# A decoder step with a 32-expert mixture: expert weights in 2 MiB pieces of 16 KB rows, and the scatter to tokens in fp32r parts

## The reference

```python
    def expert_block(args):
        xblk, e = args
        gu = xblk.astype(F32) @ w_gate_up[e].astype(F32) + b_gate_up[e].astype(F32)
        gate, up = gu[:, :D_FF], gu[:, D_FF:]
        gate = jnp.minimum(gate, SWIGLU_LIMIT)
        up = jnp.clip(up, -SWIGLU_LIMIT, SWIGLU_LIMIT)
        glu = gate * jax.nn.sigmoid(SWIGLU_ALPHA * gate)
        return ((up + 1.0) * glu) @ w_down[e].astype(F32) + b_down[e].astype(F32)

    yb = lax.map(expert_block, (xb, block_expert)).reshape(n_rows, -1)
    y = jax.ops.segment_sum(yb * gate_of_row[:, None], token_of_row, num_segments=T + 1)[:T]
```

## Time and profile before

| | us |
|---|---|
| median of 3 runs | 1326.84 |
| the 3 runs | 1319.71, 1326.84, 1328.22 |
| the profiled execution's own time | 1317.78 |
| its span, first to last instruction | 1316.1 |
| PE busy | 1264.1 (96%) |
| DMA, 400 to 1200 us | 421 GB/s at a busy share of 1.01 |

### The profile page before, as it was taken

The page is one execution under the profiler, slowest core; times in us unless marked ns, Lnnn a source line. Parts: engine busy times, 40 slices in busy tenths (PEclk is TensorE's granted clock), DMA queues, the critical chain, the costliest instruction groups (busy, mean ns, idle before and its releaser), DMA issues.

```text
span 1316.1 us, 18528 instructions
## 1 busy us (share of the span) xinstructions
PE 1264.1 (96%) x7834; PEld 570.1 (43%) x7834; DVE 396.4 (30%) x828; ACT 236.5 (18%) x500; POOL 30.9 (2%) x81
## 2 busy tenths in 40 slices
PE   7999999999999999999999999999999999998896
PEld 5777878854533333333333333333333333332232
DVE  2266756645411222122122213112221212121123
ACT  2114243411312011111111111111111111111112
POOL 6000000000010000000000000000000000000000
PEclk9999699999999999999999999999999999999999
DMA  9732111272599999999999999999999999999995
GB/s 266 165 97 65 33 42 67 67 271 74 195 399 422 421 421 420 420 422 420 420 421 421 420 420 421 420 421 423 420 420 420 421 421 421 421 420 420 422 410 188
DMA packets 77212, 436.91 MB, mean 332 GB/s; under 512 B 11892, under 2 KB 27319, under 8 KB 32072
## 3 DMA queue, kind: packets, MB, share of 16 engines
q1 hardware_dynamic: 75048, 431.11, 81.3%
q0 software_dynamic: 1040, 3.54, 0.9%
q10 hardware_dynamic: 1040, 1.05, 0.3%
HBM read 430.79 MB, written 4.89 MB: 331 GB/s over the span
## 4 chain that ended last, share of the span: by engine, by line
PE 72%; DMA 26%; DVE 1%; issue 1%; SPq 0%; ACT 0%; ACTq 0%; DVEq 0%
PE bank L1330 22%; DMA ring<-in_w_gate_up 17%; PE bank L1353 11%; PE bank L731 11%; DMA ring<-in_w_down 8%; PE bank L1312 6%; PE bank L1383 5%; PE bank L1136 3%; PE bank L1344 2%; PE bank L911 1%; PE bank L1372 1%; PE bank L859 1%; PE bank L758 1%; PE bank L888 0%; PE bank L955 0%
## 5 line engine op out<-in xcount | busy, mean ns | idle before, releaser
L1330 PE MATMUL bank<-ring,mix 128*64 128x512 f32 x2048 | 473.2, 598 | 16.4 <-DMA ring<-in_w_gate_up 16.0
L1330 PEld LDWEIGHTS bank<-ring,mix 128*64 128x64 f32 x2048 | 136.9, 136 | 320.7 <-issue 275.8
L1353 PE MATMUL bank<-ring,mix 128*64 128x512 f32 x1024 | 234.0, 598 | 8.0 <-DMA ring<-in_w_down 8.0
L2408 DVE TENSOR_TENSOR mix<-bank,w2a 128x512 f32<-128x512 f32 x32 | 22.1, 692 | 470.0 <-PE bank L1344 470.0
L731 PE MATMUL bank<-hTb,ring 128*128 128x320 f32 (+1 forms) x480 | 141.4, 451 | 0.0
L1353 PEld LDWEIGHTS bank<-ring,mix 128*64 128x64 f32 x1024 | 68.1, 136 | 135.3 <-issue 122.5
L1764 ACT ACTIVATE mix<-bank,par 128x256 f32<-128x256 f32 x64 | 26.9, 471 | 523.9 <-PE bank L1312 523.8
L2439 DVE TENSOR_TENSOR mix<-mix,bank 128x512 f32<-128x512 f32 x70 | 48.2, 688 | 233.7 <-PE bank L1383 233.7
L1312 PE MATMUL bank<-mix,hx 128*128 128x256 f32 (+1 forms) x384 | 110.3, 413 | 0.7 <-DVE mix L2312 0.7
L731 PEld LDWEIGHTS bank<-hTb,ring 128*128 128x128 f32 x480 | 92.1, 196 | 39.7 <-issue 4.3
L1383 PE MATMUL bank<-mix 128*128 128x512 f32 (+3 forms) x204 | 88.9, 625 | 1.5 <-DVE mix L2501 0.9
(11 more groups left out here) (382 smaller groups left out, 846.0 us busy)
## 6 DMA issues: line engine op xcount, KB each, us to landing
ring<-in_w_gate_up SPq DMA_DIRECT2D x256, 1024.0 KB, 26.1
ring<-in_w_down SPq DMA_DIRECT2D x64, 1024.0 KB, 23.4
ring<-in_w_down SPq DMA_DIRECT2D x32, 2048.0 KB, 23.8
ring<-in_w_in SPq DMA_DIRECT2D x14, 1024.0 KB, 5.8
ring<-in_w_out SPq DMA_DIRECT2D x2, 2048.0 KB, 9.5
hx<-in_x_prompt SPq DMA_DIRECT2D x4, 512.0 KB, 5.1
out<-ring POOLq DMA_DIRECT2D x1, 2048.0 KB, 11.9
ring<-in_w_in ACTq DMA_DIRECT2D x1, 1024.0 KB, 9.9
```

Of the source, the lines that this page charges most:

```text
L1330: last_ = mm(b_[64 * half:64 * half + 64, :], xg[:, e // 4 % 2, t0:t0 + CAP], w32[i][:, o + NCOL * half:o + NCOL * half + NCOL], start=(i ...
L1353: last_ = mm(bD[r:r + 64, :], lhs, w[:, o:o + NCOL], start=(c == 0), stop=(c == KT - 1))
```

## The change

Weights now come in 192 pieces of 2 MiB, all with rows of 16 KB in one partition: 4 up and 2 down pieces per expert. Row p of an up piece holds input rows 2p and 2p+1, so `gather` reads every second column of `h` (`rows_of`). There are 8 slots (`wslot`): six in `ring`, and two in `mix`, the mixer's memory; what lived there is moved, and the sample states that POOL writes out (`sout`) no longer lie in the ring. Piece k waits for `w_used` of piece k-8 and nothing else. Four pieces are issued after `Y0`, one after `fold` 1, three after `xo` 5. The load of the up bias stands behind the first four, that of the last norm's gain behind all weights.

The scatter's 0/1 matrix no longer holds the gates. The gate of each slot is made a column by a small product (`slot_gates`, three matmuls of 2 columns) and copied out by DVE (`gate_columns`); ACT multiplies the expert's output by it when it copies it out as an fp32r value (`y_high`), and DVE stores what is left (`down_low`, `y_low`). A scatter unit is then two fp32r matmuls, high and low, for units 1 to 4, and four for unit 0, which is now a full tile of 128 rows with zeros at the sides. `turn_gates` is three transposes for a pair, where it was six.

For the last expert the second half of the up weights comes after the down weights of expert 30, in SP's order and in PE's; all of the scatter of experts 28 and 29 is done in its first half. `swiglu` works on `upv` and `sg` in PSUM.

```diff
-PIECE = 2 * DFF
+PIECE = 4 * DFF
 NPAIR, NQUAD = NE // 2, NE // 4
-NGU, NDN = KT, KT // 2
-NPC = NGU + NDN
-REGION = [6, 7, 8, 11, 3, 0, 1, 4, 5, 2, 9, 10]
+NGU, NDN, NWS = 4, 2, 8
...
+def weight_pieces():
+
+    out = [("up", 0, j) for j in range(NGU)]
+    for e in range(1, NE):
+        early = NGU // 2 if e == NE - 1 else NGU
+        out += [("up", e, j) for j in range(early)]
+        out += [("down", e - 1, j) for j in range(NDN)]
+        out += [("up", e, j) for j in range(early, NGU)]
+    return out + [("down", NE - 1, j) for j in range(NDN)]
+
+
+PIECES = weight_pieces()
+PLACE = {x: k for k, x in enumerate(PIECES)}
...
+        yhb = later("y_high", 1024, F32R)
+        ylb = later("y_low", 1024, F32R)
+        later("y_pad", KT * NTP - 2048, F32)
+        scatb = later("slot_rows", 6 * P, F32R)
...
-        sout = at(4096, 2048).rearrange("p (b j k) -> p b j k", b=4, j=4)
+        sout = [t.rearrange("p (j k) -> p j k", j=4) for t in (mix[:, 0:512], mix[:, 512:1024], hTb[:, KT * NTP - 1024:KT * NTP - 512], hTb[:, KT * NTP - 512:KT * NTP])]
...
+        wslot = [at(2048 * n, PIECE) for n in (6, 8, 10, 2, 0, 4)] + [mix[:, 13 * W5 - PIECE * n:13 * W5 - PIECE * n + PIECE] for n in (1, 2)]
...
+            wgu = A["w_gate_up"][0].rearrange("e (j p r) n -> p e j (r n)", j=NGU, r=2)
+            wdn = A["w_down"][0].rearrange("e (h p q) n -> p e h (q n)", h=NDN, q=4)
+
+            def load_piece(k):
+
+                kind, e, j = PIECES[k]
+                if k >= NWS:
+                    sync.wait_ge(S("w_used"), k - NWS + 1)
+                load(wslot[k % NWS], wgu[:, e, j, :] if kind == "up" else wdn[:, e, j, :], f"w{k % NWS}_in")
 
             sync.wait_ge(S("unit_filled"), U("Y0", 2))
-            load_up(0, 0, range(5))
+            for k in range(4):
+                load_piece(k)
+            load(brows, bg, "brow_in")
...
             sync.wait_ge(S("unit_filled"), U("fold", 1))
-            load_up(0, 0, range(5, 7))
+            load_piece(4)
             sync.wait_ge(S("unit_filled"), U("xo", 5))
-            load_up(0, 0, range(7, NGU))
-            load_down(0, 0, range(1))
...
+            for k in range(5, len(PIECES)):
...
+                load_piece(k)
...
+            def rows_of(tile_, c):
+
+                return h[0:TN[tile_], tile_, 256 * (c // 2) + c % 2:256 * (c // 2) + 256:2]
+
             def gather_chunk(o, c, tiles, first):
 
                 for tile_ in tiles:
-                    last_ = mm(o, h[0:tn_, tile_, P * c:P * c + P], sel[0:tn_, tile_, :], start=(first and tile_ == TORD[0]),
+                    last_ = mm(o, rows_of(tile_, c), sel[tile_][0:TN[tile_], :], start=(first and tile_ == TORD[0]),
                                stop=(tile_ == TORD[2]), skip_group_check=True)
                 return last_
...
+            def slot_gates(p):
...
+                for tile_ in TORD:
+                    tn_ = TN[tile_]
+                    last_ = mm(bY[1][:, 0:2], selg[0:tn_, tile_, :, :].rearrange("p n s -> p (n s)"), gate[0:tn_, tile_, 2 * p:2 * p + 2],
+                               start=(tile_ == TORD[0]), stop=(tile_ == TORD[2]))
+                last_.then_inc(S("gates_turned"), 1)
+
+            def split_rows(o, u, r, stop, gs_=None):
 
                 tile_, half = OUT[u]
-                tn_, to_ = TN[tile_], TOFF[tile_]
+                for y_ in (yhir, ylor):
+                    for g in gs_ or ((0, 1) if tile_ == 2 else (half,)):
+                        last_ = mm(o[:, :], scatr[r[g], g, P * tile_:P * tile_ + P], y_[r[g], g, :], start=(y_ is yhir and g == half),
+                                   stop=(stop and y_ is ylor), skip_group_check=True)
+                return last_
+
...
+            def up_chunks(e, c0, c1):
+
+                q, part, p = e // 4, e % 4, (e - 3) // 2
+                for c in range(c0, c1):
+                    if part == 0 and c % 2 == 0:
+                        pe.wait_ge(S("xg_ready"), 4 * q + c // 2 + 1)
+                    up(e, c)
+                    if e == 0 and 1 <= c <= 4:
+                        sample_states(c - 1)
+                    if e == 2 and c == 0:
+                        gates_turned()
+                    if e % 2 and 1 < e < NE - 1:
+                        if c == 0:
+                            if e == 3:
+                                pe.wait_ge(S("bdr_in"), 16)
+                            turn_gates(p, p + 1)
+                        if 2 <= c <= 6:
+                            scatter(p, c - 2)
+                    if c == 7 and q + 1 < NQUAD:
+                        gather(q + 1, part)
+                    if c == 7 and e % 2:
+                        slot_gates((e - 1) // 2)
+
...
+            last_e, last_p = NE - 1, NPAIR - 1
+            pe.wait_ge(S("gu_read"), 2 * last_e)
+            up(last_e, 0)
+            turn_gates(last_p - 1, last_p)
+            up(last_e, 1)
+            scatter(last_p - 1, 0)
+            scatter(last_p - 1, 1)
+            up(last_e, 2)
+            scatter(last_p - 1, 2)
+            scatter(last_p - 1, 3)
+            up(last_e, 3)
+            scatter(last_p - 1, 4)
+            slot_gates(last_p)
+            pe.wait_ge(S("h1_ready"), last_e)
+            pe.wait_ge(S("y_read"), last_e - 1)
+            for j in range(NDN):
+                down(last_e - 1, j)
...
+            ends = (bX, bY[0], bY[1], bG, bU)
+            turn_gates(last_p, NPAIR + 1)
+            for c in range(4, KT):
+                up(last_e, c)
+            pe.wait_ge(S("scat_ready"), NPAIR)
+            pe.wait_ge(S("y_read"), last_e)
             pe.wait_ge(S("xg_ready"), NE)
-            pe.wait_ge(S("g1"), NE)
-            pe.wait_ge(S("ut_read"), NE)
-            ends = (bX, bG, bU, bGT, bUT)
-            for u in range(5):
-                last = token_rows(ends[u], u, lambda g: slice(64 * g, 64 * g + 64), True, False)
+            pe.wait_ge(S("gates_out"), NPAIR)
+            split_rows(ends[0], 0, even, False, (0,)).then_inc(S("half_rows"), 1)
+            for u in (1, 2):
+                split_rows(ends[u], u, even, False)
+            pe.wait_ge(S("half_rows"), 1)
+            split_rows(ends[0], 0, even, False, (1,))
+            turn_up(last_e)
+            for u in (3, 4):
+                last = split_rows(ends[u], u, even, False)
             last.then_inc(S("scattered"), 1)
             pe.wait_ge(S("h1_ready"), NE)
             for j in range(NDN):
-                down(NE - 1, j)
+                down(last_e, j)
             pe.wait_ge(S("scattered"), 5 * NPAIR - 4)
             pe.wait_ge(S("y_read"), NE + 1)
             for u in range(5):
-                token_rows(ends[u], u, lambda g: slice(64 - 64 * g, P - 64 * g), False, True).then_inc(S("scattered"), 1)
+                whole_rows(ends[u], u, scat, yhi, odd, False, True).then_inc(S("scattered"), 1)
...
-                cp(ytk[0:64, g, :], banks[2][0:64, :])
-                cp(ytk[64:128, 1 - g, :], banks[2][64:128, :]).then_inc(S("y_read"), 1)
+                for r, k in ((slice(0, 64), g), (slice(64, 128), 1 - g)):
+                    ins = a(yhir[r, k, :], banks[2][r, :], ACT.Copy, scale=gc[r, g:g + 1])
+                ins.then_inc(S("y_high"), 1)
...
+                b = banks[6]
+                if p == 0:
+                    a(scatr[:, 0, NT:NT + 64], b[:, 0:64], ACT.Copy, scale=0.0)
+                    a(scatr[:, 1, NT - 64:NT], b[:, 0:64], ACT.Copy, scale=0.0)
+                cp(scatr[:, 0, 0:NT], b[:, 0:NT])
+                for r in (0, 64):
+                    cp(scatr[r:r + 64, 1, 0:NT - 64], b[64 - r:P - r, 0:NT - 64])
+                    ins = cp(scatr[r:r + 64, 1, NT:NT + 64], b[64 - r:P - r, NT - 64:NT])
+                ins.then_inc(S("scat_ready"), 1)
...
+            def down_low(e):
+
+                dve.wait_ge(S("y_high"), e + 1)
+                g = e % 2
+                for r, k in ((slice(0, 64), g), (slice(64, 128), 1 - g)):
+                    ins = v.scalar_tensor_tensor(out=ylor[r, k, :], in0=banks[2][r, :], scalar=gc[r, g:g + 1], in1=yhif[r, k, :],
+                                                 op0=ALU.mult, op1=ALU.subtract)
+                signal(ins, "y_read")
+
+            def gate_columns(p):
+
+                dve.wait_ge(S("gates_turned"), p + 1)
+                if p:
+                    dve.wait_ge(S("y_high"), 2 * p)
+                    dve.wait_ge(S("y_read"), 2 * p)
+                b = banks[7]
+                for x in range(2):
+                    r = slice(64 * x, 64 * x + 64)
+                    for y in range(2):
+                        ins = v.tensor_copy(gc[64 * y:64 * y + 64, x:x + 1], b[r, x:x + 1])
+                signal(ins, "gates_out")
 
...
-                v.tensor_tensor(halves(upv), halves(banks[4][:, :]), bias(e, 1), ALU.add).then_inc(S("ut_read"), 1)
+                up_ = banks[4][:, :]
+                v.tensor_tensor(halves(up_), halves(up_), bias(e, 1), ALU.add).then_inc(S("ut_read"), 1)
```

(48 more changed lines are left out.)

329 lines of the change are left out of this document (153 added, 176 removed).

## The result

The changed kernel takes 1306.26 us (median of 4 runs, 1303.53 to 1307.99), the kernel before 1323.28 (4 runs, three of them those shown above): ratio 0.9867, 95% interval 0.9821 to 0.9914, 17 us faster. Time and sign lie inside what I gave; the gain is less than half of it.

The account below looks back on a forecast made before the run. DMA was taken to set the pace, with PE only 3% behind. The last weight at 1258.5 plus 22.7 gave a span of 1281.2, 1282.9 in the profiled execution; 5 added gave 1288 us, range 1272 to 1312.

Parts of the forecast that it names:

- time of a 2 MiB piece: Weight stream: a piece with 16 KB rows takes 4.88 us, against 4.98 at 421 GB/s.
- PE's pair: PE's work for two experts: 57.86 us becomes 57.0, against 58.6 for DMA.
- PE's own limit: PE's time without weight waits, through the first four chunks of expert 31: reached at 1253.5 us.
- D: Landing of the last weight: 352.6 + 2.0 + 6.0 + 184 x 4.88 = 1258.5 us.
- the head start of the slots: Before expert 0: all 16 MiB landed before 348.97 us, seven MiB more than before, worth 17.4 us less 1.8.
- the price of the scatter of a pair: PE's scatter: twelve fp32r matmuls of 0.30 and five shape changes, 4.35 us, 1.3 less per pair.
- Rows 4: Profile of the kernel before: 425 and 429 GB/s in 9 us around the 16 KB piece, 417 to 420 without it.
- the two are level: Last expert, after four chunks: PE's own limit gives 1253.5 us, DMA's chain D - 4.0 = 1254.5.
- The rival of the middling fp32r: Scatter: at 0.53 us per fp32r matmul PE's pair is 59.7, above DMA; time near 1325 us; chance 0.07.
- the end: From last weight to end of span: D + 22.7 = 1281.2 us, against 17.6 behind the last weight before.
- The reordering: Last expert's order: costs about 5 us, since down(31)'s weights are there before `h1` is.
- Rows of 16 KB bring little: Rival on the weight stream: 4.98 us per piece, D 18.4 later, time 1306 us; chance 0.17.

Follow-up runs that it names:

- DMA halved: Changed kernel with every piece from the ninth on loading only the first 8 KB of each 16 KB row, PE's work unchanged: 1288.20 us.
- PE lightened: Changed kernel without the low part's scatter matmuls and with two of three token tiles in each later gather, DMA unchanged: 1298.50 us.
- the plain order with its end rearranged: Changed kernel with the last expert ordered like the others, gate column before swiglu, down(31) ahead of the scatter's first half: 1298.07 us.

## Why the prediction was off

Against its own steps, in the profiled executions:

| step | forecast | measured |
|---|---|---|
| start of expert 0 | 348.97 | 353.66 |
| time of a 2 MiB piece | 4.88 | 4.91 |
| PE's pair | 57.0 | 57.04 |
| PE's own limit, from the start of expert 0 | 931 | 934.6 (DMA halved) |
| first piece of expert 31 usable | D - 34.2 = 1224.3 | 1241.5 |
| last weight landed | D = 1258.5 | 1277.1 |
| first piece of expert 31 to the end | 56.9 | 63.8 |
| span | 1281.2 | 1305.4 |

The step that failed is the size of D, the landing of the last weight, and with it that of the gain. The stream of weights ran 17 us later than my sum, and the end behind it took 7 us more than I counted. The mechanism was right.

**Right.** That DMA sets the end and PE stands close behind it; that rows of 16 KB raise the rate; that the head start of the slots is gained in full, all eight pieces having landed at 351.9, before PE starts; the price of the scatter of a pair (4 x 0.66 + 1.13 and five changes of shape, 4.5 against 4.35) and of the gate column (0.85 against 1.0); that ACT's and DVE's new links stay hidden inside the experts: none is among PE's waits before the last one.

**Wrong: D, by 17 us.** Counted at the first piece of expert 31, where PE waits for it. The trace records when each of the sixteen parts of a piece lands, and this places the loss. 4.7 us are the mixer's start, which differs between runs of one kernel; my sum hung on one profile of before, and that one had an early start. 5.0 us more are lost by the time that the 31st piece is complete, at 482.5, where my sum has 472.8. I had allowed 8 us between the first freed slot and a full stream. But DMA moved 342 GB/s from 380 to 390 and 372 from 460 to 482, at shares of 0.89 and 0.92. The first experts free their slots in bursts, with gathers, transposes and scatters between; with PE lightened it moved 429 and 428 there, and the piece came 3.8 us sooner after the start of expert 0. The last 7.4 us are in the 154 pieces from there on, which took 759.0 us, 4.93 each and not 4.88. Rows 4 read with sharp edges gave 4.83, and the long mean 4.98; I chose near the middle, and the far reading of the same rows (4.91, all of the 9 us) was nearly right, since 427 GB/s is 4.91. The 0.02 beyond it is in part this: the sixteen parts of a piece land ever further apart, 2.5 us from first to last for the 31st piece (479.99 to 482.52), 7.0 for the first piece of expert 31 (1234.52 to 1241.48), and PE waits for the last, which a byte rate does not show. Why they drift apart I don't know.

**Wrong: "the two are level".** The step said PE would be at 1253.5 where DMA is at 1254.5. PE's side was right within 4 us. DMA's was D, so with D late they were 17 us apart: the halved kernel measures it (934.6 against 951.7). The rival of the middling fp32r was priced from the same level, and so too high.

**Wrong: the end, by 7 us.** Three blocks of 32 entries cost 4.6 us more than counted, with the clock at its lower level for a part of each; I took all durations at the upper one, from rows without a stand before them. The Trainium skill ("TensorE: Matmul & The Clock Gate", What's actually happening) describes a clock gate with two levels that falls back when the engine is idle, and the trace of this kernel agrees: granted 0.59 to 0.80 in the stretches named above. The last section has a stand after which it did not fall. 3.1 us more: I let down(30) start when its own last piece had landed, but PE comes to it only after the first half of up(31) and the scatter, 14.2 us after that first piece. The scatter's units gave 0.9 back.

**Luck.** Between the profiled executions my sum was 25 us off, 1282.9 against 1307.65. The median came within 18 because I had added 5 us from profile to median, and this time the profile lay 1.4 above the median. The time inside my range owes something to that.

**The reordering.** I put it at -5 us for the kernel; undone it gives 3 to 4 by the medians. The stand of 4.1 us for the high part, the low part and the selection, which I had in the count as 1.2, 1.4 and 1.5, "all of which PE now waits for", is the part that can be had back by moving the transposes, and the clock behind it comes back too.

**The order of the rivals.** "Rows of 16 KB bring little" (1306) gave the time that was measured, for the wrong reason: the rows do bring 12 us. The runs show 427 against 420 GB/s, 1.7%. By the three cycles per packet that the Trainium skill states ("DMA: Bandwidth & Descriptors", Why small descriptors are slow (HBM only)) a doubled row would gain 0.6%, an estimate: the measurement decides, and it is three times as much.

Where the gain of 17 us comes from, by what undoing each part costs: rows 12 to 13, slots 9, fp32r 3, last expert -3 to -4, which add to about 21. That they add to more than 17 is within the spread of the runs, and the parts overlap, since each is bound by the same DMA stream.

## What to carry to other kernels

When two engines run nearly level for a thousand microseconds, the time is a little more than the larger of the two sums: here PE's bursts cost the DMA stream 3.4 us. Lighten one's load and then the other's, and both limits are nearly known. A byte rate is not yet a landing: a piece counts when its slowest part is there. A rate read from short stretches of a longer stream has the edges as its error; 0.03 us per piece was 5.5 us here. A stand of PE of some microseconds on the path may cost twice, once itself and once in the clock of the matmuls behind it: here blocks of 7.0 us took 8.6. And before profiles of two runs are compared, look at the granted clock ahead of the part that was changed.

## What the runs showed of the hardware

The 32 entries of down(31) took 7.02 us in the plain order with its end rearranged, and 8.57 in the changed kernel. In the first PE had stood 3.16 us before the three transposes ahead of them, in the second 2.75 us; but in the first the granted clock stayed at 1.00 throughout:

```profile
1262.00:1280.00 18.00, 14.84 (x71) 5.48 (x73) 5.82 (x12) 5.09 (x11) 0.00 (x0) 1.00 0.63 253
```

So the longer stand left the clock where it was and the shorter one brought it down, as did the 1.75 us of 1250 to 1256, and which one does I could not tell beforehand.

Two fp32r matmuls of 128 by 128 by 512 cost 0.66 us, a float32 one 1.06. A packet of 16 KB took 614 ns, two of 8 KB 626. The sixteen parts of a 2 MiB piece landed 7 us apart near the end of a stream of some 900 us; with DMA halved, and so idle a third of the time, 0.85 us. And the mixer, nearly the same work in all kernels, took from 348.6 to 362.2 us, mostly by how long the clock was at its lower level: a spread as large as what the largest part of this change is worth.
